# Two-layer hybrid decoder step on one core: the layer norm behind the 31-tap convolution is done in two halves of the tokens, and the first four slabs of the projection after it share one pass

## The reference, cut to what matters

```python
def conformer_conv(x, hist, norm_g, w_pw1, b_pw1, conv_w, conv_b, ln_g, ln_b, w_pw2):
    a, g = jnp.split(rmsnorm(x, norm_g) @ w_pw1 + b_pw1, 2, axis=-1)
    u = a * jax.nn.sigmoid(g)
    y, new_hist = causal_dwconv(u, hist, conv_w)          # 31 taps, per channel
    y = layernorm(y + conv_b, ln_g, ln_b)                 # over the 1024 channels
    return jax.nn.silu(y) @ w_pw2, new_hist

def layernorm(x, g, b):
    mu = jnp.mean(xf, axis=-1, keepdims=True)
    xc = xf - mu
    y = xc * lax.rsqrt(jnp.mean(xc * xc, axis=-1, keepdims=True) + EPS)
    return y * g + b
```

## Time and profile before

| | |
|---|---|
| median of three runs | 1469.98 us |
| span of the profiled execution | 1461.8 us |
| mean granted TensorE clock | 0.989 |
| TensorE busy | 1395.3 us, 95% |
| DVE, ACT, POOL busy | 720.4, 479.2, 596.9 us |
| wait of TensorE for the first `h_l` of `pw2` (L1827) | 6.5 us |

### The profile page before, as it was taken

The page is one execution under the profiler, slowest core; times in us unless marked ns, Lnnn a source line. Parts: engine busy times, 40 slices in busy tenths (PEclk is TensorE's granted clock), DMA queues, the critical chain, the costliest instruction groups (busy, mean ns, idle before and its releaser), DMA issues.

```text
span 1461.8 us, 34670 instructions
## 1 busy us (share of the span) xinstructions
PE 1395.3 (95%) x14005; PEld 1299.8 (89%) x14005; DVE 720.4 (49%) x1256; ACT 479.2 (33%) x706; POOL 596.9 (41%) x329
## 2 busy tenths in 40 slices
PE   6998998988999999999999999988999999999998
PEld 5896767767999999999999977757999999999998
DVE  5646888874535443024442376667365430144411
ACT  4375333322333222222223321227433321222221
POOL 3322333322426554445543364422255554355441
PEclk9999999999999999999999999999999999999999
DMA  6417899979323222333312566542223323332122
GB/s 185 130 54 243 296 327 322 366 270 307 94 64 96 86 79 87 94 89 90 90 57 69 143 164 157 148 115 60 69 87 90 90 76 90 101 87 86 54 84 74
DMA packets 246246, 192.56 MB, mean 132 GB/s; under 512 B 12129, under 2 KB 205106, under 8 KB 246058
## 3 DMA queue, kind: packets, MB, share of 16 engines
q1 hardware_dynamic: 244561, 188.31, 41.9%
q10 hardware_dynamic: 1181, 1.44, 0.4%
q0 software_dynamic: 400, 1.32, 0.3%
HBM read 173.03 MB, written 6.04 MB: 122 GB/s over the span
## 4 chain that ended last, share of the span: by engine, by line
PE 74%; DVE 3%; issue 2%; ACT 1%; DMA 0%; POOL 0%; SPq 0%; ACTq 0%; DVEq 0%; POOLq 0%
PE banks L1810 64%; PE banks L2243 2%; PE banks L2076 2%; PE banks L1827 1%; PE banks L2015 1%; PE banks L1957 1%; PE banks L2192 1%; DMA u_sh<-u 0%; DVE k_grp L1300 0%; SPq L610 0%; ACTq L1106 0%; PE banks L2048 0%; PE banks L1965 0%; PE banks L2246 0%; DVE sb L1363 0%
## 5 line engine op out<-in xcount | busy, mean ns | idle before, releaser
L683 POOL TENSOR_TENSOR w_l<-w_raw,w_h 128x1024 fp32r<-128x1024 f32 (+2 forms) x195 | 439.3, 2255 | 411.9 <-ACT w_h L830 397.1
L1810 PE MATMUL banks<-xa_h,w_h 128*128 128x272 f32 x1856 | 388.1, 290 | 4.4 <-DVE tmp L1633 3.3
L1810 PE MATMUL banks<-xa_h,w_l 128*128 128x272 f32 x1856 | 385.2, 289 | 0.0
L1810 PE MATMUL banks<-xa_l,w_h 128*128 128x272 f32 x1856 | 383.6, 288 | 0.0
L1810 PEld LDWEIGHTS banks<-xa_h,w_h 128*128 128x128 f32 x1856 | 292.9, 189 | 6.7 <-issue 5.5
L1810 PEld LDWEIGHTS banks<-xa_l,w_h 128*128 128x128 f32 x1856 | 292.3, 189 | 0.0
L1810 PEld LDWEIGHTS banks<-xa_h,w_l 128*128 128x128 f32 x1856 | 290.4, 189 | 0.0
L830 ACT ACTIVATE w_h<-w_raw 128x1024 fp32r<-128x1024 f32 (+2 forms) x193 | 185.1, 961 | 200.2 <-PE banks L1810 199.9
L1810 PE MATMUL banks<-h_h,w_h 128*128 128x272 f32 x928 | 193.1, 289 | 0.3 <-DVE x L1572 0.3
L1810 PE MATMUL banks<-h_h,w_l 128*128 128x272 f32 x928 | 192.6, 289 | 0.0
L1810 PE MATMUL banks<-h_l,w_h 128*128 128x272 f32 x928 | 191.9, 288 | 0.0
(11 more groups left out here) (302 smaller groups left out, 1650.8 us busy)
## 6 DMA issues: line engine op xcount, KB each, us to landing
w_raw<-in_w_up SPq DMA_DIRECT2D x88, 512.0 KB, 3.7
k_grp<-in_cache_k SPq DMA_DIRECT2D x128, 256.0 KB, 4.4
v_pg<-in_cache_v SPq DMA_DIRECT2D x120, 256.0 KB, 5.1
w_raw<-in_w_in SPq DMA_DIRECT2D x24, 512.0 KB, 6.4
w_raw<-in_w_down SPq DMA_DIRECT2D x32, 384.0 KB, 3.1
w_raw<-in_w_pw SPq DMA_DIRECT2D x24, 512.0 KB, 3.7
w_raw<-in_w_down SPq DMA_DIRECT2D x32, 320.0 KB, 3.0
w_raw<-in_w_out SPq DMA_DIRECT2D x8, 512.0 KB, 5.6
```

What stands on the lines that cost most here:

```text
L683: g.tensor_tensor(w_l[:, slot, 0:n], w_raw[:, slot, 0:n], w_h[:, slot, 0:n].bitcast(F32), ALU.subtract).then_inc(s_lo, 1)
L1810: ins = mm(out[:, half, 0:HT], w, v[:, half * HT:(half + 1) * HT], start=first and t == 0 and n == 0, stop=last and t == phase.tiles - 1 a ...
```

## The change

It does five things.

- **Pivot earlier.** It is taken from chunks 0 to 4 (`LN_PIVOT`), after the first slab of `pw1`'s last turn. The subtractions and squares of the first chunks move into the last turn's chunks, on DVE and ACT. The last turn of `pw1` is written out (`last_turn`) in place of a pass of the loop.
- **Chunk 7 in two halves of the tokens.** TensorE first convolves tokens 0 to 271 (into bank 7), then 272 to 511 and the samples (bank 6). Everything of the norm behind it is done for half 0, then for half 1.
- **Sums with tokens on partitions.** The data are the stationary operand and a single column of ones is the moving one (`ln_sums`): 12 matmuls of one column per half, in place of three sums of 2 x 272 columns. The results are 128x3. DVE takes the root there by three Newton steps (`inverse_root`: 14 instructions of 128x3 in a chain). TensorE spreads offset and inverse root back over the partitions (`spread`: 3 matmuls each). ACT's ln and exp and their tables are gone.
- **Four slabs side by side.** For half 0 TensorE multiplies each chunk into four slabs (banks 0 to 3), for half 1 into banks 4 to 7. The sums of half 1 stand after two chunks of half 0, the spreads of half 1 after five. All four slots of weights are split beforehand.
- **Behind it.** DVE adds the four slabs to x and then does their norm work; the history rows are turned after slab 4.

```diff
@@ DVE @@
-            for m in range(DC - 1):
-                V.tensor_tensor(yc[:, m, :], yc[:, m, :], pivot[:, :], ALU.subtract).then_inc(s_xc, 1)
-                if m >= 2:
-                    squares_added(m - 1)
...
-            V.scalar_tensor_tensor(halves(inv_std), gview(1), 1.0 / D, halves(off_sq), ALU.mult, ALU.subtract)\
-             .then_inc(s_var, 1)
...
+            chunk(ph["pw1"].turns - 1, 0, True, first_six, two_more)
+            chunk(ph["pw1"].turns - 1, 1, False, first_seven, squares_too)
+            def inverse_root(half):
...
+                dve.wait_ge(s_lns, 2 * half + 2)
+                V.scalar_tensor_tensor(neg, sums_at(half, 1, 0, 3), -0.5 / D, sq_off, ALU.mult, ALU.add).then_inc(s_dve, 1)
...
+                for step in range(3):
+                    V.tensor_tensor(t, y, y, ALU.mult).then_inc(s_dve, 1)
+                    stepped()
+                    V.tensor_tensor(t, t, neg, ALU.mult).then_inc(s_dve, 1)
+                    stepped()
...
+            for e in range(2 * DC + 1):
+                if e < 2 * DC:
...
+                    V.tensor_tensor(half_of(yc[:, m, :], half), half_of(yc[:, m, :], half), inv_of[half], ALU.mult)\
+                     .then_inc(s_ty, 1)
+                if e == 0:
+                    last_about_pivot(1)
+                if e + 2 < 2 * DC:
+                    if e + 2 == DC:
+                        dve.wait_ge(s_bsp, 2)
+                    centred(e + 2)
+                if e:
...
+                    V.tensor_tensor(half_of(h_l[:, m, :], half), half_of(tmp[:, m % 2, :], half),
+                                    half_of(h_h[:, m, :], half).bitcast(F32), ALU.subtract).then_inc(s_hlo, 1)
+                if e == 4:
+                    inverse_root(1)
@@ ACT @@
-            A(inv_std, inv_std, ACT.Ln, bias=eps[:, :]).then_inc(s_rt, 1)
-            A(inv_std, inv_std, ACT.Exp, scale=-0.5).then_inc(s_r, 1)
...
+                if e == 6:
+                    act.wait_ge(s_spr, 4)
+                    for to, at in zip((off_of[1], inv_of[1]), spread_at[1]):
+                        A(to, banks[:, at, 0:HT], ACT.Copy).then_inc(s_bsp, 1)
@@ TensorE @@
+            def last_turn():
+                p, i = ph["pw1"], ph["pw1"].turns - 1
+                slab(p, i, 0, xa)
+                pe.wait_ge(s_ss, ADD["mean"] + 1 + LN_PIVOT)
+                for half in range(2):
+                    ins = mm(psum_s[:, half, 64:64 + HT], ones[:, :], ssum[:, half * HT:(half + 1) * HT], start=True, stop=True)
+                ins.then_inc(s_piv, 1)
...
+                    for n in range(3):
+                        at = tokens(half, n)
+                        mm(sums_at(half, what, n), some[:, at:at + P], ones[:, 0:1], start=True, stop=False)
+                        ins = mm(sums_at(half, what, n), last[:, at:at + P], ones[:, 0:1], start=False, stop=True)
...
+            last_conv(0, range(8)).then_inc(s_cvl, 1)
+            pe.wait_ge(s_cvr, c)
+            last_conv(1, range(2))
+            pe.wait_ge(s_free, ph["pw1"].group1)
+            ln_sums(0)
+            last_conv(1, range(2, 5))
+            spread(0, 0)
+            last_conv(1, range(5, 8))
+            last_samples().then_inc(s_cvl, 1)
+            spread(0, 1)
...
+            for t in range(DC):
+                if t == 2:
+                    ln_sums(1)
+                if t == 5:
+                    spread(1, 0)
+                    spread(1, 1)
+                pe.wait_ge(s_hlo, HB["pw2"] + t + 1)
+                for j in range(4):
...
+                    part(0, j, t)
```

More of the change, by code:

```diff
@@ L1111, in turn @@
                     ahead(split_high, ph["pw1"], i, j, last)
+                    if last and j >= 2:
+                        for m in ((2,), (3, 4))[j - 2]:
+                            squared(m)
                     if j % 2:
@@ L1696, in chunk @@
                 scaled(ua[:, b, :], ph["pw1"].slab(i, 2 * b), 0)
+                if first:
+                    first()
                 dve.wait_ge(s_slab, ph["pw1"].slab(i, 2 * b + 1) + 1)
@@ new lines, in _, with added @@
+            clear_sum(SUM["pw2"])
+            both = banks[:, :, :].rearrange("p (h m) t -> p m h t", h=2)
+            def added(m, src):
+                dve.wait_ge(s_slab, ph["pw2"].slab0 + m + 1)
+                V.tensor_tensor(halves(x[:, m, :]), src, halves(x[:, m, :]), ALU.add).then_inc(s_xnew, 1)
+            for m in range(4):
+                added(m, both[:, m, :, 0:HT])
+            dve.wait_ge(s_xnew, XN["pw2"] + 4)
+            for m in range(4):
+                norm_work("pw2", m, m % 2)
@@ L1782, in _ @@
+            for m in range(4, DC):
+                added(m, gview(m % 2))
+                dve.wait_ge(s_xnew, XN["pw2"] + m + 1)
+                norm_work("pw2", m, m % 2)
             ffn(1)
@@ L1792, in _, with slab @@
             hid = lambda t: (h_h[:, t, :], h_l[:, t, :])
-            def slab(phase, i, j, moving, ready=None):
+            def slab(phase, i, j, moving, ready=None, free=None):
                 first, last = j % phase.per_group == 0, j % phase.per_group == phase.per_group - 1
@@ L2147, in _, with gemm @@
             ins.then_inc(s_misc, 1)
-            def gemm(phase, moving, ready, between=None, after_two=None, then=None, late=None):
+            def gemm(phase, moving, ready, between=None, after_two=None, then=None, late=None, ended=None):
                 seen = set()
@@ L2156, in once @@
                         ready(k)
-                if phase is ph["pw2"]:
-                    pe.wait_ge(s_var, SQ["var"] + 1)
-                    two_slabs(phase, moving, once)
-                for j in range(2 if phase is ph["pw2"] else 0, 4):
+                for j in range(4):
                     slab(phase, 0, j, moving, once)
@@ L2167, in gemm @@
                     then()
-                with pe.Fori(1, phase.turns - (1 if late else 0)) as i:
+                with pe.Fori(1, phase.turns - (1 if late or ended else 0)) as i:
                     for j in range(4):
@@ L2255, in conv_before @@
                 pe_conv(i * 2 + (b - 1), 1 - b, i + (b - 1))
-            gemm(ph["pw1"], xa, xa_ready(NORM["down01"]), sums("down01"), conv_before)
-            pe.wait_ge(s_ss, 9 * ADD["mean"] + DC)
-            pe.wait_ge(s_free, ph["pw1"].group1)
-            for half in range(2):
-                ins = mm(pair[0][:, half, 0:HT], ones[:, :], ssum[:, half * HT:(half + 1) * HT], start=True, stop=True)
-            ins.then_inc(s_piv, 1)
-            pe.wait_ge(s_pivd, 1)
-            for half in range(2):
-                mm(pair[0][:, half, 0:HT], ones[:, :], ssum[:, half * HT:(half + 1) * HT], start=True, stop=False)
@@ new lines, in _, with last_conv @@
+            gemm(ph["pw1"], xa, xa_ready(NORM["down01"]), sums("down01"), conv_before, ended=last_turn)
+            def last_conv(half, steps):
+                out, t0, t1 = (banks[:, 7, :], 0, HT) if half == 0 else (banks[:, 6, :], HT, TP)
+                for step in steps:
+                    at = max(4 * step, t0)
+                    for q in range(4):
+                        ins = mm(out[32 * q:32 * q + 32, at:t1], w_sh[1][:, q * 8 + 7 - step, :],
+                                 u_sh[1][:, q, at - 4 * step:t1 - 4 * step], start=step == 0, stop=step == 7)
+                return ins
@@ new lines, in spread @@
+            def spread(half, what):
+                pe.wait_ge((s_off, s_inv)[what], half + 1)
+                for n in range(3):
+                    at = n * P
+                    sub = ident[:, :] if n < 2 else ident[:, 3 * P - HT:]
+                    ins = mm(banks[:, spread_at[half][what], at:min(at + P, HT)],
+                             ln[:, half, (0, 3)[what], n:n + 1].to_broadcast([P, P]), sub, start=True, stop=True)
+                ins.then_inc(s_spr, 1)
+            c = DC - 1
@@ new lines, in _, with part @@
+            spread(0, 1)
+            p = ph["pw2"]
+            def part(half, j, t):
+                wh, wl = w_h[:, j, t * P:(t + 1) * P], w_l[:, j, t * P:(t + 1) * P]
+                for n, (w, v) in enumerate(((wh, h_h), (wh, h_l), (wl, h_h))):
+                    ins = mm(banks[:, 4 * half + j, 0:HT], w, half_of(v[:, t, :], half), start=t == 0 and n == 0,
+                             stop=t == DC - 1 and n == 2)
+                return ins
+            for t in range(DC):
[5 more added lines that the diff above has]
+                pe.wait_ge(s_hlo, HB["pw2"] + t + 1)
+                for j in range(4):
+                    if t == 0:
+                        pe.wait_ge(s_lo, p.slab(0, j) + 1)
+                    part(0, j, t)
```

295 lines of the change are left out of this document (185 added, 110 removed).

## The result

| | kernel before | changed kernel |
|---|---|---|
| median of four runs, us | 1467.76 | 1481.8 |
| lowest to highest, us | 1463.07 to 1470.7 | 1477.08 to 1483.34 |
| span of the profiled execution, us | 1461.8 | 1481.3 |
| mean granted TensorE clock | 0.989 | 0.982 |

The changed kernel is slower: ratio 1.0088, 95% interval 1.0068 to 1.0109, or 10 to 16 us, 12.9 in the middle (the two medians of the table are 14.0 us apart, inside that interval).

The account below looks back on a forecast made before the run. TensorE's own list was taken to bound the kernel; terms moved the next phase from 1045.66 to 1052.7, +7.0 us, giving span 1468.8 and, 8.2 above it, median 1477.0; range 1466 to 1484, the forecast's own 1473 to 1480.

Parts of the forecast that it names:

- rival D: TensorE's clock falls several times: three more low stretches of 1.85 us, +12.6 us, 1482.6; chance 0.20.
- Pivot in the last turn, +0.8: Before the last convolution: pivot sum adds 1.1 us to `pw1`'s last turn, one loop pass less saves 0.3.
- four (2.6 us) into the 3.16 us before 963.27: Four moved DVE operations, 2.6 us, fit DVE's 3.16 us wait for chunk 7's second slab; delay of u taken as 0.
- Last convolution, 3.7 us at half clock: Chunk 7's convolution, half 0: 3.5 us of work starts at 1.2 GHz after 7 us idle, taking 5.35 us.
- Column sums 2.75, spreads 0.9: TensorE's norm work: 24 one-column instructions at 0.115 us, 2.75 us per half; six spread instructions at 0.15, 0.9 us.
- The dependent small operations: DVE's root: 11 dependent operations 0.27 us apart, 3.0 us, hidden by half 1 of the convolution.
- Wait at the fifth tile 1.4, at the sixth 1.85, one low stretch 1.85: Half 0's products: TensorE waits for DVE's `h_l` before t4 and t5, and runs one more stretch at half clock.
- Slab 4's weights 1.6, history rows 1.05, SP's queue 0: Behind the four slabs: TensorE waits 1.6 us for split weights, history rows add 1.05, later next weights cost nothing.
- What the old two-slab pass cost: Old products in `pw2`: preceded by a 6.53 us wait, begun at 1.2 GHz for 3.7 us, costing 1.85 us.
- B: TensorE's sums, spreads and root steps are cheap and the clock holds: 1470.8; chance 0.21.
- C: Half 0 starts `pw2` during half 1's work and TensorE never waits in between: -5 us, 1465; chance 0.13.

Follow-up runs that it names:

- e1: Changed kernel with four VectorE operations moved behind u of chunk 7 and ScalarE's squares of chunks 3 and 4 behind its shifts; ratio 1.0060 to the kernel before.
- e2: Kernel before plus four unused VectorE additions of two SBUF operands in the wait for the projection's last slab; ratio 1.0029, local +3.39 us.
- e3: Kernel before plus four unused VectorE operations reading one PSUM operand in the wait for the projection's last slab; ratio 0.9996, local +0.09 us.
- f1: Kernel before with 78 unread matmuls put in TensorE's waits; ratio 0.9997, local -1.01 us.
- f2: Changed kernel with 72 unread matmuls ahead of the last convolution and 14 ahead of the first product; ratio 1.0066 to the kernel before.
- g4: Changed kernel with four VectorE operations behind chunk 7's u, half 1's sums, root and spreads earlier, 48 unread matmuls before the last convolution; ratio 1.0020 to the kernel before.

## Why the prediction was right, and where it was not

Forecast 1477.0, measured 1481.8, inside the range of 1466 to 1484, but outside the forecast's own 1473 to 1480 and next to rival D's 1482.6. As a change it was +7.0 against +12.9 us; the times lie closer because the kernel before came out at 1467.76 with its fourth run, 2.2 us under the median that I had added to. So the direction is earned by the terms below, and that the time fell into the range is in part luck: a term that I had at nothing cost 4 us, and the width that I allowed for D took it in. I also gave more chance to a difference within half a per cent (0.50) than to more (0.42), and it was 0.88%. Between the marks the sum was 4.1 us short.

- *Pivot in the last turn, +0.8.* Measured +0.70.
- *"four (2.6 us) into the 3.16 us before 963.27 ... If the last cover were too small, u of chunk 7 and its DMAs would be late by the rest; I take 0."* This step failed, and it is nearly all of the miss between the marks. The four took 5.8 us, not 2.6, and the gap was 2.0 us, not 3.16, so u was 3.8 us late and the last convolution came 3.99 us later. At 2.6 us the four would have been 0.6 late; POOL's two operations made the other 3.2. e1 takes them away (3.7 of it back), e2 puts their like into the kernel before (+3.39), e3 the same number without a second SBUF operand (+0.09). I had read VectorE's gap and not POOL's list beside it.
- *Last convolution, 3.7 us at half clock.* It was 5.4, +0.9; it goes with the longer idle time.
- *Column sums 2.75, spreads 0.9.* Measured 2.77 and 0.77, in half 1 2.98 and 1.4 for two. The dependent small operations were 0.197 us apart, not 0.27; hidden, as forecast.
- *Wait at the fifth tile 1.4, at the sixth 1.85, one low stretch 1.85.* No wait at the fifth, 1.60 at the sixth, and 6.8 us at half clock, 3.4. The products at half clock ran slower than VectorE's `h_l`, so TensorE didn't wait at the fifth. Together 5.0 against 5.1, which is luck: one term was not there, another was twice its size.
- *Slab 4's weights 1.6, history rows 1.05, SP's queue 0.* Measured 1.41 and 1.04, and no wait of TensorE for the next weights.
- *What the old two-slab pass cost.* I gave the new kernel a gain there only through the wait of 6.53 us. f1 shows that the low stretch in the old pass cost nothing.

Of the rivals B and C are out: a column matmul costs 0.11 us a pass and the clock did fall. D, three more low stretches, isn't what happened: there were two, as in the forecast, but longer, worth 6.1 us against 3.7.

The change as a whole: it takes 2.8 us off the way to the first product and pays for it with two sets of column sums, two spreads and two waits in the middle of the products, and with u of chunk 7.

## What to carry over

A gap of VectorE is cover only for operations that can run in it: those with two SBUF operands need POOL idle too (and so did the one-operand tap L1773), so add POOL's remaining instruction to their time, or put there what reads PSUM. Ask of a low stretch whose pace it lies behind before you pay for it or fill it; and where light work follows the wait, filling it may only move the fall of the clock, as in f2 and g4.

## What the runs showed of the hardware

- A VectorE operation with two SBUF operands of 128x544 took 2.28 us instead of 0.72 beside a POOL operation of 128x1024; those that read PSUM were not held (four with one operand in 2.84 us, and one with a PSUM and an SBUF operand in 0.71). The other way round, POOL's operation took 4.49 instead of 2.40 us where VectorE's taps ran on without a gap.
- TensorE's clock stood at 0.50 in the last 7.7 us of an 11 us wait and in the next 5.4 us of work; with 72 unread matmuls in the wait it was 1.00 there, and stood at 0.56 over 988 to 991, behind the one-column sums and light work that followed.
- A float32 matmul with one moving column and 128 weight columns took 0.223 us (two passes).
